# First block of a two-block kernel: attention by groups of heads written between the next group's projections, cross-attention output by rows of its weight, head norm on eight rows

## The reference, cut to what matters

```python
for i in range(2):
    u = rms_norm(h, mix_pre_g[i])
    # A: 16 heads of 64: q, k, v = split(u @ w_in); rope on q and k; three dilated windows
    #    combined by their softmax sums (here one softmax over 256 keys with a log-count mask)
    # B: 8 heads, each (softmax(Q1 K1') - lam * softmax(Q2 K2')) V with 128 value columns,
    #    then rms_norm over each head's 128 columns, times sub_g and a constant
    y = mixer(u) @ w_out
    h = h + rms_norm(y, mix_post_g[i])
    u = rms_norm(h, mem_pre_g[i])
    # memory: 4 heads of 256; k, v = split(rms_norm(mem, mem_kv_g[i]) @ wkv)
    y = merge(softmax((u @ wq) k' / 16) v) @ wo
    h = h + rms_norm(y, mem_post_g[i])
    u = rms_norm(h, ffn_pre_g[i])
    y = (silu(g) * up) @ w_down          # g, up = split(u @ w_gate_up), 2816 wide
    h = h + rms_norm(y, ffn_post_g[i])
```

## Time and profile before

| what | us |
|---|---|
| three runs | 2472.34, 2481.1, 2491.87 |
| the profiled execution, time | 2482.18 |
| its span, first to last instruction | 2480.3 |
| PE busy | 2079.6 (84%) |
| DVE busy | 981.4 (40%) |
| ACT busy | 731.2 (29%) |
| POOL busy | 671.1 (27%) |
| granted TensorE clock, mean | 0.896 |

### The profile page before, as it was taken

The page is one execution under the profiler, slowest core; times in us unless marked ns, Lnnn a source line. Parts: engine busy times, 40 slices in busy tenths (PEclk is TensorE's granted clock), DMA queues, the critical chain, the costliest instruction groups (busy, mean ns, idle before and its releaser), DMA issues.

```text
span 2480.3 us, 35494 instructions
## 1 busy us (share of the span) xinstructions
PE 2079.6 (84%) x14031; PEld 1635.2 (66%) x14035; DVE 981.4 (40%) x1805; ACT 731.2 (29%) x1146; POOL 671.1 (27%) x224
## 2 busy tenths in 40 slices
PE   4979979998769989979999956758799999569855
PEld 4949879998659889977768743324477687434423
DVE  2870335516672245316644341111367442411212
ACT  4444443444444343422312111212223121112211
POOL 2625626785435448820002000000000020000000
PEclk8989989999889989989999867879899998679977
DMA  5404425554323335543310247998413002477793
GB/s 166 155 32 135 137 70 174 178 175 136 102 68 120 119 123 183 174 131 122 122 48 1 103 185 317 388 420 312 144 69 135 35 2 102 196 312 288 289 421 131
DMA packets 202118, 404.52 MB, mean 163 GB/s; under 512 B 18483, under 2 KB 152006, under 8 KB 177270
## 3 DMA queue, kind: packets, MB, share of 16 engines
q1 hardware_dynamic: 198230, 388.85, 42.8%
q0 software_dynamic: 3744, 13.63, 1.5%
HBM read 399.18 MB, written 3.28 MB: 162 GB/s over the span
## 4 chain that ended last, share of the span: by engine, by line
PE 68%; DVE 11%; DMA 9%; ACT 3%; DVEq 3%; issue 2%; POOL 1%; SPq 1%; ACTq 1%; POOLq 0%
PE ps L1127 9%; PE ps L888 8%; PE ps L889 8%; PE ps L890 8%; PE ps L1434 7%; DMA weight_ring<-in_w 5%; DMA acts<-in_w 4%; PE ps L1354 2%; PE ps L1456 2%; DVEq L1936 2%; PE ps L918 2%; PE ps L1143 2%; PE ps L928 1%; POOL weight_ring L1893 1%; PE ps L1209 1%
## 5 line engine op out<-in xcount | busy, mean ns | idle before, releaser
L1893 POOL TENSOR_TENSOR weight_ring<-weight_ring 128x2048 fp32r<-128x2048 f32 x132 | 602.8, 4583 | 468.0 <-ACT weight_ring L1522 468.0
L888 PE MATMUL ps<-weight_ring 128*128 128x256 f32 x1824 | 530.4, 291 | 61.2 <-DVE acts L1964 24.2
L890 PE MATMUL ps<-weight_ring 128*128 128x256 f32 x1568 | 442.8, 282 | 0.0
L889 PE MATMUL ps<-acts,weight_ring 128*128 128x256 f32 x1472 | 419.5, 285 | 0.0
L888 PEld LDWEIGHTS ps<-weight_ring 128*128 128x128 f32 x1824 | 348.9, 191 | 70.5 <-issue 27.5
L890 PEld LDWEIGHTS ps<-weight_ring 128*128 128x128 f32 x1568 | 302.4, 193 | 0.0
L889 PEld LDWEIGHTS ps<-acts,weight_ring 128*128 128x128 f32 x1472 | 282.7, 192 | 3.5 <-issue 3.1
L1522 ACT ACTIVATE weight_ring<-weight_ring 128x2048 fp32r<-128x2048 f32 x132 | 246.6, 1885 | 97.9 <-PE ps L890 87.9
L1434 PE MATMUL ps<-weight_ring,x_g 128*32 128x512 f32 x1056 | 188.9, 661 | 93.2 <-DMA acts<-in_w 56.2
L1127 PE MATMUL ps<-acts,weight_ring 128*128 128x272 f32 x896 | 216.5, 402 | 5.0 <-ACTq L1756 5.0
L1127 PEld LDWEIGHTS ps<-acts,weight_ring 128*128 128x128 f32 x896 | 174.5, 195 | 43.8 <-issue 6.8
(11 more groups left out here) (435 smaller groups left out, 3770.4 us busy)
## 6 DMA issues: line engine op xcount, KB each, us to landing
weight_ring<-in_w SPq DMA_DIRECT2D x132, 1024.0 KB, 19.6
weight_ring<-in_w_gate_up SPq DMA_DIRECT2D x44, 1024.0 KB, 5.1
acts<-in_w SPq DMA_DIRECT2D x40, 1024.0 KB, 25.3
weight_ring<-in_w_in SPq DMA_DIRECT2D x16, 2048.0 KB, 8.5
h_area<-in_w SPq DMA_DIRECT2D x20, 1024.0 KB, 27.9
weight_ring<-in_x_wkv SPq DMA_DIRECT2D x16, 1024.0 KB, 5.4
weight_ring<-in_w_down SPq DMA_DIRECT2D x16, 1024.0 KB, 5.1
weight_ring<-in_a_w_in SPq DMA_DIRECT2D x12, 1024.0 KB, 7.0
```

Of the source, the lines that this page charges most:

```text
L888: nc.tensor.matmul(o, wh, xh, start=start, stop=False)
L889: nc.tensor.matmul(o, wh, xr, start=False, stop=False)
L890: return nc.tensor.matmul(o, wr, xh, start=False, stop=stop)
L1893: nc.gpsimd.tensor_tensor(r12(w), w, r12(high[:, n % HIGH, 0:k * 256]).bitcast(F32), ALU.subtract).then_inc(rest_ready, 1)
```

## The change

**Mixer by groups.** A table `mixer_order` replaces the sequence of eight q/k chunks, four v chunks and all heads. Chunks are cut in halves of 24 matmuls. First come the q, k and v chunk of group 0; then, four times, the heads of one group (four for A, two for B) stand between the six half chunks of the next group's q, k and v, or, the fourth time, between those of mk. All engines' lists follow this table; the leads of `ahead` are no longer used for the order (`attention(l, kind, what, m)` does one step).

**Memory input.** ACT makes the high parts right after the last v chunk (8 copies of 128x256), and DVE the rests (`memory_rest`, 8 instructions) where mk begins.

**Maxima of A.** One `tensor_tensor_reduce` for each half (128x256) masks, scales and reduces at once, in place of three instructions.

**Memory's attention.** `memory_order` puts xq chunks and output chunks between its steps. The output is projected by 256 rows of its weight, so that chunk m needs head m alone; it adds into four banks (0 to 3) that are full after the last chunk.

**Head norm.** The sums of squares of eight heads are gathered on eight rows (`ss`), root and reciprocal are 8x256, and a matmul spreads them to 128 partitions (`sub`).

**Rests in pieces.** POOL makes each chunk's rest in four instructions of 128x512, and PE waits for the piece that it needs (`rest_of`).

```diff
+        def mixer_order(kind):
+
+            per = 4 if kind == "A" else 2
+            order = [("qk", 0, 0), ("qk", 0, 1), ("norm",), ("qk", 4, 0), ("rot", 0), ("qk", 4, 1), ("rtok",), ("v", 0, 0), ("rot", 4), ("v", 0, 1)]
+            for g in range(1, 5):
+                q0, q1, k0, k1, v0, v1 = [("qk", g, 0), ("qk", g, 1), ("qk", 4 + g, 0), ("qk", 4 + g, 1), ("v", g, 0), ("v", g, 1)] if g < 4 else \
+                    [("mk", c, j) for c in range(3) for j in range(2)]
+                rots = [[("rot", g)], [("rot", 4 + g)]] if g < 4 else [[], []]
+                m = per * (g - 1)
+                S, T, V = ([(what, m + i) for i in range(per)] for what in "STV")
+                if kind == "A":
+                    order += [S[0], S[1], q0, q1, T[0], S[2], k0, *rots[0], V[0], T[1], S[3], k1, V[1], T[2], v0, *rots[1], V[2], T[3], v1, V[3]]
+                else:
+                    order += [S[0], q0, S[1], q1, k0, *rots[0], T[0], k1, V[0], T[1], v0, *rots[1], V[1], v1]
+            if kind == "B":
+                return order[:-3] + [V[1], ("mk", 2, 0), ("ss",), ("mk", 2, 1), ("mk", 3, 0), ("sub",), ("mk", 3, 1)]
+            return order + [("mk", 3, 0), ("mk", 3, 1)]
+
+        def memory_order():
+
+            return [("xq", 0), ("xq", 1), ("S", 0), ("xq", 2), ("S", 1), ("T", 0), ("xq", 3), ("T", 1), ("S", 2), ("V", 0), ("S", 3),
+                    ("xo", 0), ("T", 2), ("V", 1), ("xo", 1), ("T", 3), ("V", 2), ("xo", 2), ("V", 3), ("xo", 3)]
...
+            def rest_of(key, k):
+
+                n = bay_of[key]
+                pe.wait_ge(rest_ready, 4 * n + min(4, -(-4 * (k + 1) // bay_order[n][0])))
...
+            def project_rows(l, m):
+
+                key = ("xo_rows", l, m)
+                w = split_weights(*key)
+                if m == 0:
+                    for c in range(4):
+                        begin("xo", l, c)
+                for c in range(4):
+                    b = tiles[("xo", l, c)][0]
+                    for nt in (2 * c, 2 * c + 1):
+                        for k in range(2):
...
+                    elif what == "ss":
+                        pe.wait_ge(sub_sq, 8)
+                        b = begin("ss")
+                        for h in range(KT):
+                            last = nc.tensor.matmul(ps[0:KT, b, 0:S1], head_of[:, 7 - h:15 - h], sq[:, h, 0:S1],
+                                                    start=(h == 0), stop=(h == KT - 1))
+                        last.then_inc(full[b], 1)
...
+                        if what == "S" and m % per == 0:
+                            pe.wait_ge(qk_ready, 8 * l + 2 * (m // per + 1))
+                        if what == "V" and m % per == 0:
+                            pe.wait_ge(v_ready, 8 * l + m // per + 1)
+                        attention(l, kind, what, m)
...
-                w = raw[:, n % RAW, 0:k * 256]
-                nc.gpsimd.tensor_tensor(r12(w), w, r12(high[:, n % HIGH, 0:k * 256]).bitcast(F32), ALU.subtract).then_inc(rest_ready, 1)
+                for a in range(4):
+                    part = slice(a * k * 64, (a + 1) * k * 64)
+                    w = raw[:, n % RAW, part]
+                    nc.gpsimd.tensor_tensor(r12(w), w, r12(high[:, n % HIGH, part]).bitcast(F32), ALU.subtract).then_inc(rest_ready, 1)
...
+            def memory_rest(l, c):
+
+                dve.wait_ge(memh_ready, 4 * l + c + 1)
                 for k in (2 * c, 2 * c + 1):
+                    ins = nc.vector.scalar_tensor_tensor(out=r12(uT[:, k, 0:S1]), in0=memn[:, k, :], scalar=gains[:, 48 + 8 * l + k:49 + 8 * l + k],
+                                                         in1=r12(uH[:, k, :]).bitcast(F32), op0=ALU.mult, op1=ALU.subtract)
+                ins.then_inc(mem_u, 1)
...
+                            for j in range(2):
+                                part = slice(j * S1, (j + 1) * S1)
+                                ins = nc.vector.tensor_tensor_reduce(out=probs[:, s, c, part], in0=src[:, part], in1=maskA[:, part], scale=-scale,
+                                                                     scalar=-NEG, op0=ALU.add, op1=ALU.min, accum_out=nmax[:, s, c, j:j + 1])
```

More of the change, by code:

```diff
@@ L473, in build @@
         turn = [0]
+        rotation = [list(range(BANKS))]
         def take(*key, bank=None):
             if bank is None:
-                bank = turn[0] % BANKS
+                bank = rotation[0][turn[0] % len(rotation[0])]
                 turn[0] += 1
@@ L541, in rotary_order, with plan_attention @@
-        def rotary_order():
-            order = []
-            for g in range(8):
-                order.append(("qk", g))
-                if g:
-                    order.append(("rot", g - 1))
-            return order + [("rot", 7)]
+        def plan_attention(l, kind, what, m):
+            if what == "S":
+                for c in range(score_tiles(kind)):
+                    take("S", l, kind, m, c)
+            elif what == "T":
+                take("T", l, kind, m)
+            elif kind != "A" or m % 2 == 0:
+                take("V", l, kind, m)
@@ L1602, in exps @@
                     nc.scalar.drain().then_inc(exp_ready, 1)
-                for m in range(min(ahead(kind), n)):
-                    exps(m)
-                for m in range(n):
+                elif what == "T":
                     b = filled("T", l, kind, m)
@@ L1609, in attention @@
                     nc.scalar.drain().then_inc(free[b], 1)
-                    if m + ahead(kind) < n:
-                        exps(m + ahead(kind))
+                elif kind == "B":
+                    act.wait_ge(o_ready, 12 + m + 1)
+                    nc.scalar.activation(sq[:, m, 0:S1], oT[:, m, 0:S1], ACT.Square).then_inc(sub_sq, 1)
             act.wait_ge(memset_done, 2)
@@ L2065, in heads_out @@
                     nc.vector.drain().then_inc(free[b], 1)
-                for m in range(min(ahead(kind), n)):
-                    maxima(m)
-                for m in range(n):
-                    normalise(m)
-                    if m + ahead(kind) < n:
-                        maxima(m + ahead(kind))
-                    if m > 1:
-                        heads_out(m - 2)
-                    if kind != "X" and m < 4:
-                        memory_input(l, m)
-                heads_out(n - 2)
-                heads_out(n - 1)
+                dict(S=maxima, T=normalise, V=heads_out)[what](m)
+            nc.vector.memset(head_of[:, :], 0.0)
+            settle()
+            nc.vector.memset(head_of[:, 7:8], 1.0)
+            settle()
             nc.vector.memset(ones[:, :], 1.0).then_inc(memset_done, 1)
```

460 lines of the change are left out of this document (247 added, 213 removed).

## The result

The changed kernel takes **2551.0 us** (median of four, 2548.2 to 2552.7) against 2484.2 of the kernel before: ratio **1.027** (1.023 to 1.032). 2522 was forecast, 2463 to 2550 the range. The direction and the place of the main losses were as forecast; the size was short by 29 us, and the time lies 1 us above the range.

What follows compares the result with a forecast made beforehand. PE was taken as the bound, busy 84% of 2480.3 us, its idle time and clock winnable. Terms 17.4 + 18.0 + 8.5 + 5.1 + 0.6 - 3.3 - 6.7 = +39.6 on 2482.18 gave 2522 us, range 2463 to 2550.

Steps and rivals of the forecast that it cites:

- T1: Mixer A, PE's wait at T of head 1, behind rotation and V0, for DVE's rotation and normalising: 4.0 us a group.
- T2: Mixer A, PE's wait at T of head 2, directly behind V1, for taking heads out and normalising: 2.1 us.
- T3: Mixer A, PE's wait at T of head 3, like that of head 1 but mostly after POOL's pieces: 2.4 us.
- mk's two together: Mixer A's fourth group, mk 0 waiting for v's copy, ACT's high part and copies, and DVE's eight new instructions: 5.0 us.
- Memory's attention: PE stalls at T0, T1 and the last three output chunks: 12.5 and 10.0 us, with clock +8.5 and +5.1.
- T0 of B: Mixer B, first T directly behind the rotation: 4.4 us free, 9.3 behind all four pieces; 7.0 charged, three times.
- T1 of B: Mixer B, T of the second head behind V0: 2.75 us with half a wait, 3.4 charged, four times.
- clock: Mixers and memory's attention: each idle us of PE costs 0.3 us more in clock, so stalls count 1.3 times.
- The free port (1): Whole kernel: POOL's pieces end before the rotation, so DVE's port is free when it matters; 2489 us, chance 0.22.
- The steady clock (2): Whole kernel: free port and the clock stays at 1.00, so the change is faster; 2466 us, chance 0.13.
- POOL as the bound (3): Chunk pairs: pieces of 1.4 us where DVE cuts in outlast PE's 11.3 us a pair; 2537 us, chance 0.07.
- The fourth: All turns: every contending DVE instruction waits for a piece; A +32, B +43, memory +18; 2566 us, chance 0.08.

Runs made afterwards that it cites:

- e2: Changed kernel with the tables reordered: half a chunk between a rotation and the next T, T of the next head before V; 2458.6 us, 0.992.
- e7: Changed kernel with POOL subtracting one column of each piece, values wrong; first block ends at 1085.1 us against 1158.7 for the changed kernel.
- e12: Changed kernel run and profiled once more, unchanged; the profiled execution took 2539.3 us, the four 2538.1 to 2551.3.
- e1: Changed kernel without late_norm's product eps_u where nothing reads it; 2547.3 us, 1.027.
- e6: Kernel before with two parts of the change: POOL's pieces and layer 1's head norm on eight rows; 2455.2 us, 0.991.
- e9: Changed kernel with mixer tables mended further, memory's attention reordered, ACT's high parts moved, eps_u made only where read; 2443.7 us, 0.985.
- e4: Kernel before with only POOL's rests in four pieces and PE waiting for the piece it needs; 2456.7 us, 0.990.
- e10: Changed kernel with POOL waiting before the fourth chunk's first piece until DVE has done late_norm; 2539.5 us, 1.025.
- e11: Changed kernel with mended tables, POOL's run broken before the fourth chunk, and DVE's own list in the memory's attention; 2427.0 us, 0.978.

## Why the prediction was short

**Right.** The place and the cause of the loss: PE meets DVE's turns too early (e2), and DVE has POOL's pieces in front of it (e7). Of mixer A, where no instruction is held (e12), +19.4 us against +17.4: idle time +12.1 (forecast 12.5). The waits of A were 3.05 to 3.43 at T1 (4.0), 2.12 at T2 (2.1), 2.14 to 2.50 at T3 (2.4), mk's two together 5.54 (5.0). Memory's attention, +9.6 and +5.8 against +8.8 and +5.4 with the tail. T0 of B, 7.4 against 7.0. The start and the feed-forwards gained as forecast, the latter more (11.4 for 6.7): no wait for POOL is left there, and clock came back with it. Of the signs, the waits at T, the 5 us before mk and the rotation instructions (1.56 and 1.59 us) came; projection o of layer 1 waited 2.35 us, not 4 to 5. The memory's terms add up to +8.65 and +5.4 by the prediction's own numbers, where its sum has 8.5 and 5.1; that is half a us.

**Failed, a term that was not in the sum: the wait of `rtok` for `late_norm`, 14 us.** The prediction walked the new table from the first group's heads on, and its row of the start is of the first chunk alone. It did not ask what the move of `rtok` from behind all q and k chunks to ahead of the first v chunk puts PE behind. Even so it would have charged one piece, 1.24 us: it took from the earlier trace rows that DVE waits for one POOL instruction at a time. That is what DVE does at the turns, but not in every execution under the unbroken run at the start. All four executions of the result took 2548 us or more; of the profiled one the hold is shown, of the other three it is only likely. An execution without it, 2539.3 us in e12, lies inside the range, still 17 us above the forecast.

**Failed, a mis-sized term: T1 of B.** 3.4 was charged, as 2.75 with half a piece; it measured 4.93 three times and 6.28 once, 7.5 us more over the four. The free part is 2.84 (e7). Two `scalar_tensor_tensor` that follow one another each waited for a piece, since POOL's chunk starts at the same point of every group; a mean over POOL's busy share is no price for something that falls at the same place each time.

**Failed, a factor: clock.** 0.3 us for each idle us came from two windows before. For B the forecast's clock term was +5; it measured +16.1. Before, 36.1 us of waits in B had cost 8.6 of it; the 45.5 forecast were to cost 13.7, and the 53.4 that came cost 8.6 + 16.1 = 24.7, 0.46 apiece. e2 against after gives 0.42 in B. In A e12 has 7.3 for the forecast 4.9.

The sum of these: 14 (hold) + 2 (A's clock) + 8 (B's stalls: T1 7.5, T0 1.2, mk 0.8, S0 0.8, less 2.4 for the head norm and V) + 11 (B's clock) + 1 (memory), less 5 in the feed-forwards and 1 at the start, are 30, the 30.4 us between +39.6 and +70.0.

**The rivals.** The free port (1) is what e7 built: its first block ends 3.5 us earlier than before, where the rival charged +7. Its prices for A (+5) and the memory of layer 0 (+7) fit e7's +4.8 and +5.6; it had B too low (0 for +4.4), and the start and feed-forwards gained 16 us for its 10. With POOL at work the port was not free. The steady clock (2) is out: it was 0.82 over B. POOL as the bound (3) is out: e2 keeps its work and saves 92 us. The fourth, every contending instruction waiting for a whole piece, gave 2566, nearer to 2551 than 2522 is, and its +43 for B is nearer to +37.1 than +18.0 is; but the mechanism is not what happened in full: at T0 of B the seven instructions lost 3.2 us together, 0.5 to 0.9 where one lost any, and B's excess was clock and T1. The rule of the Trainium skill, page "SBUF — State Buffer", section "Who interferes with whom", that the one who comes second is blocked until the other's instruction ends, agrees with these rows (0.88 and 0.90 us lost by the two rotation instructions, less than a piece of 1.24), and L2218, which reads one input from PSUM, took 0.69 in e12 at 59.11, in the midst of POOL's run, and 0.69 in e7. A wait over several POOL instructions does not follow from it; the measured 12.3 to 25.5 us decide.

## What to carry to other kernels

An interleaving fills waits only where the engine that hands over has the time of a whole filler between being asked and being needed. Lay the table out for that engine: put its turns (rotation, normalising, taking out) each behind a different filler. The same instructions cost 78 us more in the first block when two turns stood together (e12 against e2). And when work moves nearer to the start of a stage, walk each wait that moves with it, small ones too: a held instruction that nothing read cost 14 us, and a product of 128x1 in its place 8.5.

## What was not expected of the hardware

- **A DVE instruction with two inputs in SBUF can wait for the whole of an unbroken run of POOL instructions.** 14.29, 13.33, 25.53 and 12.31 us in four profiles (after, e1, e6, e9), each ending with POOL's run within 0.3 us; in three others with the same start (e12, e2, e4) DVE got in between the pieces and lost at most 1.1 us at a time. It befell a `scalar_tensor_tensor` of 128x256 and a `tensor_tensor` of 128x1 alike. It occurred only at the start, where POOL runs 24 to 36 pieces without a wait; POOL's later unbroken runs of 36, in the feed-forwards, met hardly any DVE instruction of this kind (one in the first of the result's profile, 1.62 us). It occurred in neither of the two profiles where the run was broken (e10, e11), but with three of seven free of it anyway, that can be chance. What decides in one execution is open.
- **Idle time costs clock on top**, 0.35 to 0.6 us for each idle us here (B of e7 against after 8.5 for 24.3; B of e2 against after 16.9 for 40.3; A of e12 against after 5.3 for 8.8), with a granted clock of 0.82 over B and 0.89 over A in the result's profile. No single factor fits all of them.
- **Cutting POOL's instruction in four costs POOL 9%** (24 pieces in 29.82 us, 4.97 for a chunk, against four whole chunks in 18.29, 4.57 each) and shortened every stage of the first block of the kernel before (e4).
